# 28 products of a zero tile put ahead of a transformer kernel's first product

## The reference, cut to what matters

```python
def _mla(x, w_in, g_q, g_kv, w_uq, w_uk, w_uv, w_o, pos):
    ...
    h = x @ w_in
    c_q = _rmsnorm(h[..., :MLA_Q_RANK], g_q)
    c_kv = _rmsnorm(h[..., MLA_Q_RANK:MLA_Q_RANK + MLA_KV_RANK], g_kv)
    k_r = _rope(h[..., MLA_Q_RANK + MLA_KV_RANK:], pos)
...
def _swa(x, w_q, sinks, w_o, k_band, v_band, rel_bias):
    ...
    bias = rel_bias[_t5_bucket(dist)].astype(jnp.float32)
```

## Time and profile before

| what | value |
|---|---|
| median of three executions | 1084.91 us (1084.87 to 1085.3) |
| the profiled execution, its own time | 1084.94 us |
| span of its trace | 1083.1 us |
| TensorE busy | 1062.9 us, 98% of the span |
| VectorE busy | 762.2 us, 70% |
| ScalarE busy | 642.2 us, 59% |
| granted TensorE clock, mean | 1.000 |

### The profile page before, as it was taken

The page is one execution under the profiler, slowest core; times in us unless marked ns, Lnnn a source line. Parts: engine busy times, 40 slices in busy tenths (PEclk is TensorE's granted clock), DMA queues, the critical chain, the costliest instruction groups (busy, mean ns, idle before and its releaser), DMA issues.

```text
span 1083.1 us, 22255 instructions
## 1 busy us (share of the span) xinstructions
PE 1062.9 (98%) x8247; PEld 958.1 (88%) x8247; DVE 762.2 (70%) x1313; ACT 642.2 (59%) x1159; POOL 10.0 (1%) x27
## 2 busy tenths in 40 slices
PE   6999999999999999999999999999999999999998
PEld 6978899989887789889988988898999979999997
DVE  5876755557796675555677778656765968777776
ACT  5876654544676774545558875445576447666663
POOL 1000000000000000000000000000000000000000
PEclk9999999999999999999999999999999999999999
DMA  9545655655665346565673543122255645656652
GB/s 356 186 156 209 192 184 192 186 183 181 205 212 151 108 156 194 178 188 178 192 226 115 165 129 109 59 80 79 79 163 171 192 156 161 209 176 190 187 187 95
DMA packets 49171, 181.76 MB, mean 168 GB/s; under 512 B 5537, under 2 KB 5697, under 8 KB 48209
## 3 DMA queue, kind: packets, MB, share of 16 engines
q1 hardware_dynamic: 46512, 168.32, 48.9%
q0 software_dynamic: 1584, 7.63, 2.3%
q10 hardware_dynamic: 1008, 4.89, 1.1%
HBM read 179.74 MB, written 1.07 MB: 167 GB/s over the span
## 4 chain that ended last, share of the span: by engine, by line
PE 89%; DVE 5%; ACT 3%; DMA 2%; issue 1%; DVEq 0%; ACTq 0%; SPq 0%
PE acc L741 28%; PE work L688 12%; PE work L692 12%; PE work L691 12%; PE acc L688 4%; PE acc L692 3%; PE acc L691 3%; ACT whi L1442 1%; DVE wlo L2055 1%; DMA sqr<-x_t 1%; PE work L726 1%; DVE res L2078 1%; DMA raw<-weights 1%; PE work L812 1%; PE work L716 1%
## 5 line engine op out<-in xcount | busy, mean ns | idle before, releaser
L2055 DVE TENSOR_TENSOR wlo<-raw,whi 128x1024 fp32r<-128x1024 f32 x319 | 388.9, 1223 | 142.5 <-ACT whi L1442 140.9
L1442 ACT ACTIVATE whi<-raw 128x1024 fp32r<-128x1024 f32 x319 | 335.8, 1056 | 121.4 <-PE acc L741 83.9
L688 PE MATMUL work<-xh,whi 128*128 128x256 f32 x1024 | 289.8, 283 | 0.6 <-ACT k_ L1783 0.2
L691 PE MATMUL work<-xl,whi 128*128 128x256 f32 x1024 | 288.8, 282 | 0.0
L692 PE MATMUL work<-xh,wlo 128*128 128x256 f32 x1024 | 288.7, 282 | 0.0
L688 PEld LDWEIGHTS work<-xh,whi 128*128 128x128 f32 x1024 | 194.2, 190 | 7.9 <-issue 2.1
L691 PEld LDWEIGHTS work<-xl,whi 128*128 128x128 f32 x1024 | 193.7, 189 | 3.5
L692 PEld LDWEIGHTS work<-xh,wlo 128*128 128x128 f32 x1024 | 194.5, 190 | 0.0
L741 PE MATMUL acc<-whi,hl 128*128 128x512 f32 x344 | 108.0, 395 | 0.0
L741 PE MATMUL acc<-wlo,hh 128*128 128x512 f32 x344 | 108.0, 395 | 0.0
L741 PE MATMUL acc<-whi,hh 128*128 128x512 f32 x344 | 108.0, 395 | 0.0
(11 more groups left out here) (456 smaller groups left out, 1635.1 us busy)
## 6 DMA issues: line engine op xcount, KB each, us to landing
raw<-weights SPq DMA_DIRECT2D x319, 512.0 KB, 3.6
gb<-ln_rows POOLq DMA_DIRECT2D x4, 1024.0 KB, 6.6
memraw<-mem_t ACTq DMA_DIRECT2D x1, 1024.0 KB, 14.8
x<-mem_tok ACTq DMA_DIRECT2D x1, 1024.0 KB, 17.7
x<-x_tok ACTq DMA_DIRECT2D x1, 1024.0 KB, 7.9
qlat<-bias_scratch POOLq DMA_DIRECT2D x1, 1024.0 KB, 11.0
qlat<-bias_scratch POOLq DMA_DIRECT2D x4, 256.0 KB, 4.0
out_tok<-res SPq DMA_DIRECT2D x4, 256.0 KB, 2.1
```

The lines of the kernel that those rows point to most:

```text
L688: a = mm(dst, whi[:, n % RING, col], hi, start=start, stop=False, skip_group_check=shared)
L691: mm(dst, whi[:, n % RING, col], lo, start=False, stop=False, skip_group_check=shared)
L1442: act_fn(whi[:, n % RING, :], raw[:, n % RING, :], ACT.Copy).then_inc(cut_hi, 1)
L2055: tt(wlo[:, n % RING, :], raw[:, n % RING, :], whi[:, n % RING, :].bitcast(F32), ALU.subtract).then_inc(cut_lo, 1)
```

## The change

Ahead of its first product TensorE waits for `zeros_set` and then issues 28 products of the zero tile into `work[3]`, the bank in which the third chunk of "in" will later start anew. The wait for `zeros_set` that stood ahead of `feature_major("ln0")` goes away, since the same engine has then passed it.

```diff
+            pe.wait_ge(sig("zeros_set"), 1)
+            zero_products(work[3], 28)
             pe.wait_ge(sig("band_loaded"), 32)
             close_result(mm(open_result(("brow", 0))[0:16, 0:384], relb[:, :], bandt[:, 0, :], start=True, stop=True), ("brow", 0))
...
             token_major("memva", 2, T, memh, meml)
-            pe.wait_ge(sig("zeros_set"), 1)
             feature_major("ln0")
```

## The result

The changed kernel took 1087.63 us (median of 15 executions, 1085.93 to 1088.9), the kernel before 1085.0 (15 executions, 1084.71 to 1085.61). The ratio is 1.0021, with an interval of [1.0014, 1.0028]: slower, by about 2.3 to 2.6 us, and outside the predicted range of 1083.3 to 1086.3.

A forecast was written before the change was run, and what follows sets the result against it. It took the start to be bound by the transfer chain to `ckvl`, not TensorE: 28 products hidden (0), small product and chunks -1.07 us, given back as +1.07 of waiting at 31.24, so 1084.9 us; range 1083.3 to 1086.3.

The forecast's parts named there:

- The lead: TensorE's early chunks: with full-rate products the second chunk starts at 14.54 instead of 15.61, 1.07 us earlier.
- The wait inside the first chunk: TensorE, now early, waits about 1 us for the cutting of x between pairs of x's chunks.
- the lead is not passed on: At stage "k" TensorE waits for `ckvl` until 31.24 as before, 1.8 us instead of 0.7; passing on had chance 0.06.
- none of them moves: ScalarE's roundings of the fifth and sixth slices (17.23, 21.73) and the copies at 22.82 keep their times.
- so a wait of 1.8 us here should leave the clock up: Ahead of stage "k": TensorE continues at full rate after the longer wait, as after 1.78 us of idleness ahead of 382.08.
- The slower rivals: Two cases at the program's start that slow the kernel, to 1087.7 us (chance 0.03) and 1087.8 us (0.04).
- Late zero products: At TensorE's start, zero products don't raise the clock and end at 12.96: +2.8, 1087.7 us; chance 0.03.
- the instruction supply: 56 more instructions make TensorE ask earlier for a block and run dry: 2.9 us by median landing, 1087.8; chance 0.04.

The follow-up runs named there:

- e8_moved_loop: Kernel before with the 28 zero products as a loop and the 1 MB transfer of the memory's tokens moved to GpSimd's queue: 1082.78 us, ratio 0.9979.
- e6_nops160: Kernel before with 160 empty instructions on TensorE ahead of its first product, no zero products: 1087.17 us, ratio 1.0021.
- e3_loop28: Changed kernel with its 28 zero products written as a loop of seven rounds of four: 1085.08 us, ratio 1.0004.
- e2_nops80: Kernel before with 80 empty instructions on TensorE ahead of its first product, no zero products: 1086.32 us, ratio 1.0011.
- e4_fill: Changed kernel with twelve more zero products ahead of the wait for `ckv_cut`: 1086.15 us.
- e9_loop_fill: Changed kernel with the 28 zero products in a loop and 8 more ahead of the wait for `ckv_cut`: 1085.08 us, ratio 0.9999.
- e5_nops24: Kernel before with 24 empty instructions on TensorE ahead of its first product, no zero products: 1085.18 us, ratio 1.0001.
- e7_moved: Kernel before with the 1 MB transfer of the memory's tokens issued by GpSimd behind the two small LoRA transfers instead of by ScalarE: 1084.84 us, ratio 0.9997.
- e1_again: Changed kernel once more without any edit, for a second trace and every execution's clock: 1087.54 us, ratio to before 1.0025.

## Why the prediction was wrong

**Right: what TensorE does.** The 28 products fit into the first wait; they ended at 8.71, earlier than the 9.2 to 9.8 of the sum, since only seven of them were 0.427 us apart (the clock rose at 4.05, after 3.05 us and not 4.0 to 5.4). The lead was 1.35 us at the second chunk (14.26 against 15.61; forecast 1.07) and 1.1 us at the end of the sixth (29.35 against 30.43 for its last product). The wait inside the first chunk was 0.33 us and not about 1: the first pair of x's chunks ended at 11.4, and the next low part was there at 11.7. Zero products do raise the clock. The Trainium skill says on its page "TensorE: Matmul & The Clock Gate", part 1, that activity releases the half rate; the trace agrees.

**Right: the lead is not passed on.** No execution of the changed kernel is shorter than any of before, and e8_moved_loop shows that the transfers stood in the way: with one of them moved the same zero products gain 2.06 us.

**The step that failed: "none of them moves".** The prediction held that the rounding of the sixth slice hangs on its transfer and on no condition of TensorE's that is still open, and so stays at 21.73. It came at 22.86. I had the instruction block among the rivals, with "one block of instructions comes in between 20 and 25 us" and the right shift of some microseconds, but asked only whether TensorE would run dry. It didn't. The block is itself a transfer: one packet of 1.08 us, in a stretch with a DMA share of 1.0, ahead of a slice on which the chain hangs. What the runs show for it: blocks at 19.8, 19.97, 19.87, 20.61 and 16.07 with reloads rounded at 22.86, 22.89, 22.80, 22.78 and 22.89; blocks at 24.35, 24.43, 23.44 and 22.90 with reloads rounded at 21.73, 22.24, 22.17 and 21.69. In time, without a fall of the clock, the first group (e6_nops160 aside, where TensorE was late) took 1086.1 to 1086.3 against 1085.0 to 1085.2. That the landing waits for one DMA engine that carries the block is argued from the sizes and not shown; the traces do not say which engine a packet used.

**The second step that failed: "so a wait of 1.8 us here should leave the clock up".** It rested on one row, 1.78 us ahead of 382.08. The wait became 2.8 to 3.0 us because of the first error, and the clock fell, by the two traces and the mean clocks, in 18 of 23 executions of the changed kernel (those over 1087 us). But even without that error it would not have held: in e3_loop28, with a wait near 2.2 us, it fell in 4 of 11. Where the wait was filled or short it fell in none of 43 (e2_nops80, e4_fill, e9_loop_fill, e5_nops24). A fall costs 1.4 us, fifteen products at half rate. That the wait is what brings it is shown by the two fillings, after which no execution has it; how long a wait must be is not: 1.78 us in one trace didn't, 2.19 did in some executions, 2.79 didn't in the first trace of the changed kernel and 2.97 did in the second.

**The sum as it should have been:** 1085.0, +1.1 for the block on the reload, +1.4 for the clock in four of five executions, gives 1086.1 without a fall and 1087.5 with one; measured median 1087.63, from 15 executions of which ten had a fall.

**The slower rivals** had the right sign for other reasons. Late zero products (0.03) were to give 1087.7 us and the instruction supply (0.04) 1087.8; both numbers lie near the measured 1087.63 by luck, since the zero products ended early and TensorE never ran dry. What happened is half of the second, the block asked for earlier, with another mechanism behind it, and a clock that falls after the longer wait was not priced at all.

**Open.** Five of the 23 executions took 1088.3 to 1088.9 us, about 1.1 us more than one fall explains, with a mean clock of 0.996 or 0.997, so they spent more time at the lower rate than one fall takes. None of them was traced, and where that time lies is not known. In e7_moved, eight of eleven executions are 1.2 us longer than the other three; TensorE bounds there, and how late its clock rises would explain it (it rose at 13.8 in the traced one, at 15.0 before, at 16.9, 16.2 and 17.6 in the versions with 80, 24 and 160 empty instructions), but only one of the eleven has a trace.

## What to carry to other kernels

Before costing added instructions at nothing because their engine is idle, look up when its next instruction blocks are fetched and what lies in the DMA queues at that time: a block that moves into a full stretch delays what the chain waits for. Work that makes an engine early only lengthens its next wait if something else bounds it, and on TensorE a longer wait can cost the clock behind it (here 1.4 us); fill such a wait, or take away what it waits for. Putting the filler in a loop gives the activity without the instructions.

## What the runs showed of the hardware that I had not expected

The granted clock's column read 1.00 from 10.82 to 14.83 before, where products were 0.213 us apart, and it reads 1.00 at the start of the other traces too, while products run at the half rate. Behind the wait of e1_again it did read 0.50, for 3.42 us. So at the start of a trace the rate has to be read from the distance between products; why the column misses it no run shows.

The clock rose at 4.05, 5.94, 5.39, 6.82, 4.78, 3.73 and 6.80 us in seven traces whose zero products all began at 1.0 to 1.1: the moment varies by 3 us from trace to trace, and by 1.9 us between the first two, which are of the same kernel. The Trainium skill says on its page "TensorE: Matmul & The Clock Gate", part 1, that the number of products at the lower rate varies from run to run; these traces agree.

An empty instruction on TensorE takes 0.07 us in a row (80 from 0.8 to 6.6, 160 from 0.8 to 12.4), a third of a zero product of 512 columns at 2.4 GHz (0.216 us).
